# Storing the hi and lo halves of the stationary activations column by column, at a stride of 8 bytes

## The reference

```python
def rms_norm(x, w):
    y = xf * lax.rsqrt(jnp.mean(xf * xf, axis=-1, keepdims=True) + EPS)
    return (y * w)

def swiglu(h, w_gate, w_up, w_down):
    return (jax.nn.silu(h @ w_gate) * (h @ w_up)) @ w_down

x = x + 0.5 * swiglu(rms_norm(x, norm_ffn1_w), ffn1_w_gate, ffn1_w_up, ffn1_w_down)
x = x + head_group_mixer(rms_norm(x, norm_mix_w), w_in, attn_sinks, ret_gn_w, w_out)
x = x + 0.5 * swiglu(rms_norm(x, norm_ffn2_w), ffn2_w_gate, ffn2_w_up, ffn2_w_down)
return rms_norm(x, norm_final_w)
```

## Time and profile before

| | |
|---|---|
| runs, us | 1823.14, 1823.10 (median 1823.12) |
| the profiled execution, us | 1823.17 |
| its span, first to last instruction, us | 1821.4 |
| mean granted TensorE clock | 0.999 of full speed |
| weight bytes read | 344.04 MB, 190 GB/s over the span |

### The profile page before, as it was taken

The page is one execution under the profiler, slowest core; times in us unless marked ns, Lnnn a source line. Parts: engine busy times, 40 slices in busy tenths (PEclk is TensorE's granted clock), DMA queues, the critical chain, the costliest instruction groups (busy, mean ns, idle before and its releaser), DMA issues.

```text
span 1821.4 us, 22695 instructions
## 1 busy us (share of the span) xinstructions
PE 1807.5 (99%) x8314; PEld 1495.8 (82%) x8314; DVE 1183.8 (65%) x1399; ACT 823.5 (45%) x986; POOL 63.6 (3%) x59
## 2 busy tenths in 40 slices
PE   9999999999999999999999999999999999999998
PEld 6888888888888888888888888888888888888886
DVE  5666676676676667544466665676676666667666
ACT  6434444443443445455555455444443443444444
POOL 0000000000000000100045000000000000000000
PEclk9999999999999999999999999999999999999999
DMA  9565565655556555555545456556556556555562
GB/s 371 194 199 185 197 194 187 199 189 191 201 185 196 195 186 187 182 167 179 163 160 185 139 176 208 194 186 203 187 191 201 185 195 197 186 199 191 189 204 93
DMA packets 175235, 346.64 MB, mean 190 GB/s; under 512 B 5984, under 2 KB 8416, under 8 KB 175072
## 3 DMA queue, kind: packets, MB, share of 16 engines
q1 hardware_dynamic: 174768, 345.61, 57.3%
q10 hardware_dynamic: 432, 0.55, 0.1%
HBM read 344.04 MB, written 2.10 MB: 190 GB/s over the span
## 4 chain that ended last, share of the span: by engine, by line
PE 98%; DVE 1%; DMA 1%; issue 0%; ACT 0%; SPq 0%; POOLq 0%; POOL 0%; DVEq 0%
PE ps L328 32%; PE ps L330 32%; PE ps L329 32%; PE ps L355 1%; DMA raw<-in_g 1%; DVE w_lo L850 0%; PE ps L475 0%; PE ps L563 0%; PE ps L574 0%; PE ps L488 0%; ACT w_hi L638 0%; PE ps L444 0%; PE ps L442 0%; PE ps L443 0%; DVE x L914 0%
## 5 line engine op out<-in xcount | busy, mean ns | idle before, releaser
L850 DVE TENSOR_TENSOR w_lo<-raw,w_hi 128x1024 fp32r<-128x1024 f32 x648 | 806.0, 1245 | 603.6 <-ACT w_hi L638 602.5
L638 ACT ACTIVATE w_hi<-raw 128x1024 fp32r<-128x1024 f32 x648 | 687.0, 1061 | 966.9 <-PE ps L330 957.1
L328 PE MATMUL ps<-w_hi,xT_hi 128*128 128x512 f32 (+1 forms) x1816 | 706.7, 389 | 1.7 <-DVE w_lo L850 1.1
L329 PE MATMUL ps<-w_lo,xT_hi 128*128 128x512 f32 (+1 forms) x1816 | 703.4, 387 | 0.0
L330 PE MATMUL ps<-w_hi,xT_lo 128*128 128x512 f32 (+1 forms) x1816 | 703.4, 387 | 0.0
L328 PEld LDWEIGHTS ps<-w_hi,xT_hi 128*128 128x128 f32 x1816 | 341.0, 188 | 72.5 <-DVE w_lo L850 1.6
L330 PEld LDWEIGHTS ps<-w_hi,xT_lo 128*128 128x128 f32 x1816 | 341.0, 188 | 70.1
L329 PEld LDWEIGHTS ps<-w_lo,xT_hi 128*128 128x128 f32 x1816 | 341.0, 188 | 68.7
L328 PE MATMUL ps<-w_hi,hT_hi 128*128 128x512 f32 x640 | 249.1, 389 | 0.0
L330 PE MATMUL ps<-w_hi,hT_lo 128*128 128x512 f32 x640 | 249.0, 389 | 0.0
L329 PE MATMUL ps<-w_lo,hT_hi 128*128 128x512 f32 x640 | 249.0, 389 | 0.0
(11 more groups left out here) (110 smaller groups left out, 499.2 us busy)
## 6 DMA issues: line engine op xcount, KB each, us to landing
raw<-in_u SPq DMA_DIRECT2D x88, 1024.0 KB, 5.1
raw<-in_d SPq DMA_DIRECT2D x88, 1024.0 KB, 4.9
raw<-in_g SPq DMA_DIRECT2D x87, 1024.0 KB, 5.1
raw<-in_w_in SPq DMA_DIRECT2D x40, 1024.0 KB, 4.9
raw<-in_w_out SPq DMA_DIRECT2D x16, 1024.0 KB, 5.0
x<-in_x SPq DMA_DIRECT2D x4, 512.0 KB, 12.6
raw<-in_w_in SPq DMA_DIRECT2D x4, 512.0 KB, 3.6
out<-proj SPq DMA_DIRECT2D x8, 256.0 KB, 2.4
```

What stands on the lines that cost most here:

```text
L328: pe.matmul(out, xh, wh, start=first and j == 0, stop=False)
L329: pe.matmul(out, xh, wl, start=False, stop=False)
L638: act.activation(dst, raw[:, s, (k % 2) * HALF:(k % 2 + 1) * HALF], ACT.Copy).then_inc(hi_ready, 1)
L850: dve.tensor_tensor(w_lo[:, k % LEAD, :, :].rearrange(flat), raw[:, k // 2, (k % 2) * HALF:(k % 2 + 1) * HALF], f32(w_hi[:, k % LEAD, :, : ...
```

## The change

The three pairs are stored as one tensor each with a last dimension of 2, and the old names become views of it. Every reader and writer keeps its line; the addresses that it steps through are 8 bytes apart. The whole diff:

```diff
-        xT_hi = sb("xT_hi", [P, KT, SEQ], F32R)
-        xT_lo = sb("xT_lo", [P, KT, SEQ], F32R)
+        xT_pair = sb("xT_pair", [P, KT, SEQ, 2], F32R)
+        xT_hi, xT_lo = xT_pair[:, :, :, 0], xT_pair[:, :, :, 1]
...
-            hT_hi = sb("hT_hi", [P, 4, SEQ], F32R, ffn)
-            hT_lo = sb("hT_lo", [P, 4, SEQ], F32R, ffn)
+            hT_pair = sb("hT_pair", [P, 4, SEQ, 2], F32R, ffn)
+            hT_hi, hT_lo = hT_pair[:, :, :, 0], hT_pair[:, :, :, 1]
...
-        attT_hi = sb("attT_hi", [P, KT // 2, SEQ], F32R)
-        attT_lo = sb("attT_lo", [P, KT // 2, SEQ], F32R)
+        attT_pair = sb("attT_pair", [P, KT // 2, SEQ, 2], F32R)
+        attT_hi, attT_lo = attT_pair[:, :, :, 0], attT_pair[:, :, :, 1]
```

## The result

The changed kernel takes 1875.1 us as the median of two runs (1871.69 and 1878.54), against 1823.1: a ratio of 1.0285 (95% interval 1.0269 to 1.0302). A later series of five runs, made for its spread, gave 1878.3 to 1878.5, ratio 1.0303 (1.0289 to 1.0317). It is slower by about 3%; 1823.5 us and no change had been forecast. The profiled execution took 1871.69 us, with a span of 1869.9.

The account below looks back on a forecast made before the run. The prediction took the number of TensorE matmuls times the distance between their starts as the bound. To the profiled 1823.17 us it added 0 for loads and 0.4 for writes, giving 1823.5 us, range 1815 to 1845.

Parts of the forecast that it names:

- What bounds the kernel: Whole kernel: number of matmuls times the distance between their starts, 7680 at 0.2267 us and 96 at 0.120, 1753 of 1821.4 us.
- The load keeps its length: Weight loads stepping 8 bytes: stream as now, record near 188 ns; at most the streaming part doubles, 102 ns more.
- I take nothing: Price of the strided weight loads: 0 us taken, from bounds of nothing and +10 us on the 96 narrow matmuls.
- right: Sign in a middle stretch: 60 loads still fit in 13.6 us; narrow matmuls 120 ns apart, load record near 188 ns.
- wrong: Sign in the middle stretch: matmul distance of 240 ns or more, or 216, so the load isn't wholly beside the matmul.
- The slower rival: All 7776 matmuls: the strided load takes read cycles from the moving operand, 240 ns apart, +104 us, 1927 us; chance 0.17.
- Its second form: Matmul distances: all of the narrow 120 ns is the load's and doubles, +114 us, 1937 us; within the 0.17 chance.
- One row for it: Slower f32 products: six of 256 columns in 1.29 us, 215 ns each, only 2 ns extra with the same 128-column loads.
- The faster rival: All 7776 matmuls: the extra 32 cycles come from the tile's layout and go, -90 us, 1733 us; chance 0.03.
- The writes: ScalarE and VectorE pieces at 8 bytes: at most +0.48 and +0.56 us per 512 columns; about +2 us together, 0.4 taken.
- the covered cases: Weight loads still hidden behind matmuls: no change, chance 0.72, or the load doubles but stays covered, 1834 us, chance 0.08.

Follow-up runs that it names:

- the table: Kernels that only measure, 36 matmuls back to back in each form, nothing of the reference computed; at 512 columns 226.9 ns at 4 bytes, 233.3 at 8.

## Why the prediction was wrong

- **What bounds the kernel** held: number of wide matmuls times their distance gives the time before and, with 233.3 for 226.7, that of the profiled execution after to within 3 us (1874.4 for 1871.7).
- **The load keeps its length** held, and more closely than its bounds: the record went from 188 to 193 ns, not to 290. What the Trainium skill says in SBUF — State Buffer, section "Door 1: The DMA port swizzle", that two accesses to a 16-byte line are enough, held for the load itself: 8 bytes add 8 ns at most to its repeat (118 against 110), 16 bytes double it (233), and the writes of ScalarE and VectorE follow the same pattern (617 and 685 ns at 8 bytes, 1107 and 1091 at 16). The same note of the Trainium skill also puts the free stride at 4 fp32, which the prediction passed over; if that means a stride of 16 bytes, the 233 ns of the load go against it.
- **The step that failed** is the one behind "I take nothing": that a load that ends in time costs nothing, so that only its length had to be priced. The sum's term for the 7680 wide matmuls was 0; it measured +6.67 ns each, 51 us. The signs that the prediction set for this step were 240 ns or more, or 216; the 233.3 to 235.6 measured lie between its "right" and its "wrong". The runs show that where and how the stationary tile lies changes the start of the next matmul although the load stays covered all the while (a record of 188 to 193 ns within 227 to 233): +5.6 ns by a shift of 4 bytes at an unchanged record, and no loss at 504, 384 or 256 columns at an unchanged stride.
- **The slower rival** had the sign and the place: the layout of the stationary tile acts on the wide matmuls. Its price was twice too high (240 ns, 1927 us), and its count of one cycle for each 16 bytes is refuted by the stride of 16 bytes (235 ns, not 267), by 32 stationary columns (232 ns, not less) and by the shift of 16 bytes. Its second form, that all of the 120 ns is the load's and doubles, is refuted by the narrow matmuls, which stayed at 120 ns. A chance of 0.17 was too low: the 32 unexplained cycles on each matmul were seen beforehand and taken as fixed, although the trace of before varied them: after each interruption the same kind of matmul, with its load covered, came 224 to 240 ns after the last before the run settled at 226.7. One row for it was also misread: the six records of the earlier trace rows are three f32 products, since each product leaves two records (12 products in the code of L574, 24 records); the 1.7 ns of extra for a record stand.
- **The faster rival** named a clash of the two read streams that another layout avoids. No layout brought the distance under the one of before.
- The sentence of the Trainium skill, TensorE: Matmul & The Clock Gate, section "Part 2: What happens when you issue a matmul", that loading the next tile takes nothing from the running matmul was given too much weight. It agrees with plain f32 (no change at 8 bytes) and with narrow fp32r matmuls; at 512 columns in fp32r the distance depends on how the next tile lies, at unchanged length of its load, for which the sentence leaves no room.
- **The writes** were bounded well (33 ns more for ScalarE on 512 elements, 4 for VectorE), and stayed hidden: TensorE's idle time before L328 grew by 0.2 us.
- **The range** 1815 to 1845 held only the covered cases; the effect was larger.

What stays open is the mechanism. That the distance depends on the stride, on the positions of both operands and on the width of the moving one, in fp32r and not in plain f32, and that a run settles at one of few distances after each interruption, fits two read streams that meet in SBUF and fall into step with each other. This is argued: no run shows the meeting itself, and none varies the moment at which a run begins. No rule was found that gives the distance in advance: a shift of 16 bytes costs 6.4 ns in the table and nothing in the kernel.

## What to carry to other kernels

When a kernel is bound by fp32r matmuls of 512 columns, lay the stationary tile out without a stride and start it, like the moving one, at a multiple of 256 bytes, and then compare the distance between matmuls in a long run (one half by its count) with 226.7 ns; 230 to 236 means that the layout costs 1.5 to 4%. A load that is hidden in time is not thereby free. A trace that seems to hold a cost fixed should be read matmul by matmul just after an interruption, where this one varied. A bare table of back-to-back matmuls gives such a price for strides in a single run, and gave that of the shift by 64 bytes to 0.1 ns; for the shift by 16 bytes it failed, so the kernel must confirm it.

## What the runs showed of the hardware that had not been expected

- At 512 columns in fp32r the distance is 544 cycles at 2.4 GHz at best and 560 or 565 at a stride of 8 bytes (233.3 and 235.6 ns); at 504 columns it is 544 for both.
- Moving a contiguous stationary tile by 4 bytes costs 5.6 ns on every matmul (232.5 against 226.9), in the kernel 10.7 us on 1920 of them.
- A load of 32 columns gives a longer distance (231.7 ns) than one of 128 (226.9).
- With the stride of 8 bytes a run of wide matmuls settles at 233.3 or at 235.6 ns after an interruption and keeps it up to the next, once for 700 us; without the stride runs settle at 226.7 after two to ten distances of 224 to 240 ns.
